# A hybrid decoder trunk on one core: sample products on GpSimd, branch A in plain float32, small copies on ScalarE

## The reference, cut to what matters

```
hn = rmsnorm(x, norm1_g) * (1 + sc1) + sh1
xr, yr, ga, gb, gate_a, gate_b = split(hn @ w_in)
xc, rc_new = causal_depthwise_conv(xr, rc_state, rg_conv_w, rg_conv_b)       # 4 taps
hseq, h_last = rg_lru(xc, h_state, ...)
ya = (gelu(yr) * hseq) @ w_branch_a
u = ga * sigmoid(gb)
v, cc_new = causal_depthwise_conv(u, cc_state, cc_dw_w, cc_dw_b)             # 31 taps
v = silu(layernorm(v, cc_ln_g, cc_ln_b))
yb = v @ w_branch_b + b_branch_b
m = sigmoid(gate_a) * ya + sigmoid(gate_b) * yb
x = x + (1 + g1) * (m @ w_out)
```

## Time and profile before

| | |
|---|---|
| median of 3 runs | 1541.03 us |
| the profiled execution | 1540.55 us |
| its span in the trace | 1538.7 us |
| TensorE matmul busy | 1349.4 us (88%) |
| VectorE busy | 890.1 us (58%) |
| ScalarE busy | 440.7 us (29%) |
| GpSimd busy | 326.2 us (21%) |
| mean granted TensorE clock | 0.936 |

### The profile page before, as it was taken

One profiled execution on the slowest core, in us unless ns is written; L12 is line 12 of the kernel. 1 busy time (PEld: TensorE's weight loads), 2 busy tenths in 40 slices (PEclk: granted clock), 3 DMA queues, 4 the chain that ended last, 5 costly groups with the idle time before them and its releaser, 6 DMA issues.

```text
span 1538.7 us, 28763 instructions
## 1 busy us (share of the span) xinstructions
PE 1349.4 (88%) x12262; PEld 1065.0 (69%) x12262; DVE 890.1 (58%) x1583; ACT 440.7 (29%) x669; POOL 326.2 (21%) x145
## 2 busy tenths in 40 slices
PE   4899996479799999995999935896899999999996
PEld 2798896379699898995997935895454444555443
DVE  3587999967744434336999998765212332212324
ACT  4234474142533332324346521422100000000001
POOL 1366667000000000005775840000100000000000
PEclk9899998789999999997999967996799999999998
DMA  9866524824396674435443447278199999999961
GB/s 398 237 241 226 212 79 130 45 96 168 100 383 239 233 256 141 151 103 122 146 151 97 137 97 73 78 238 335 29 380 370 382 385 382 388 370 372 383 253 35
DMA packets 169954, 332.37 MB, mean 216 GB/s; under 512 B 58480, under 2 KB 133616, under 8 KB 161808
## 3 DMA queue, kind: packets, MB, share of 16 engines
q1 hardware_dynamic: 168576, 327.68, 64.3%
q0 software_dynamic: 1296, 3.54, 0.7%
HBM read 326.06 MB, written 5.13 MB: 215 GB/s over the span
## 4 chain that ended last, share of the span: by engine, by line
PE 67%; DVE 29%; DMA 2%; ACT 1%; issue 1%; POOL 0%; DVEq 0%; SPq 0%; ACTq 0%
PE ps L741 17%; PE ps L542 11%; PE ps L543 10%; PE ps L544 10%; DVE ps L1084 9%; PE ps L765 8%; DVE prod L1105 4%; PE ps L568 2%; PE ps L729 2%; PE ps L584 2%; DVE v L1106 2%; PE ps L576 1%; DVE ps L1081 1%; DMA raw<-in_stream 1%; DVE xc L1250 1%
## 5 line engine op out<-in xcount | busy, mean ns | idle before, releaser
L542 PE MATMUL ps<-xn_hi,whi 128*128 128x320 f32 x1248 | 393.8, 316 | 36.7 <-DVE xn_lo L1032 33.8
L496 POOL TENSOR_TENSOR wlo<-raw,whi 128x1024 fp32r<-128x1024 f32 x104 | 295.5, 2861 | 612.5 <-ACT whi L798 612.5
L543 PE MATMUL ps<-xn_lo,whi 128*128 128x320 f32 x1248 | 388.8, 312 | 0.0
L544 PE MATMUL ps<-xn_hi,wlo 128*128 128x320 f32 x1248 | 388.6, 311 | 0.0
L798 ACT ACTIVATE whi<-raw 128x1024 fp32r<-128x1024 f32 x210 | 221.2, 1056 | 230.1 <-PE ps L544 175.2
L542 PEld LDWEIGHTS ps<-xn_hi,whi 128*128 128x128 f32 x1248 | 237.1, 190 | 54.5 <-issue 33.3
L543 PEld LDWEIGHTS ps<-xn_lo,whi 128*128 128x128 f32 x1248 | 237.4, 190 | 0.2
L544 PEld LDWEIGHTS ps<-xn_hi,wlo 128*128 128x128 f32 x1248 | 237.1, 190 | 0.0
L1032 DVE TENSOR_TENSOR wlo<-raw,whi 128x1024 fp32r<-128x1024 f32 x106 | 128.7, 1221 | 146.2 <-ACT whi L798 146.1
L1084 DVE SCALAR_TENSOR_TENSOR ps<-upad,cols,ps 128x256 f32<-128x256 f32 x464 | 183.5, 478 | 0.0
L542 PE MATMUL ps<-q_hi,whi 128*128 128x320 f32 x256 | 85.8, 335 | 92.5 <-DVE q_lo L1032 58.1
(11 more groups left out here) (232 smaller groups left out, 1510.3 us busy)
## 6 DMA issues: line engine op xcount, KB each, us to landing
raw<-in_stream SPq DMA_DIRECT2D x210, 512.0 KB, 3.7
gbuf<-in_moe SPq DMA_DIRECT2D x36, 1408.0 KB, 13.2
dbuf<-in_moe SPq DMA_DIRECT2D x36, 1408.0 KB, 14.6
ubuf<-in_moe SPq DMA_DIRECT2D x36, 1408.0 KB, 15.2
ada<-in_ada SPq DMA_DIRECT2D x24, 2048.0 KB, 8.3
out_cc<-upad SPq DMA_DIRECT2D x18, 120.0 KB, 13.1
wrg<-in_wrg SPq DMA_DIRECT2D x2, 1024.0 KB, 20.5
upad<-in_cc SPq DMA_DIRECT2D x16, 120.0 KB, 3.4
```

The source lines that it names most:

```text
L496: e.tensor_tensor(wlo[:, s, :], raw[:, s, :], whi[:, s, :].bitcast(F32), ALU.subtract).then_inc(lo_pool, 1)
L542: e.matmul(out, w[0], x2[0], start=start, stop=False)
L543: e.matmul(out, w[0], x2[1], start=False, stop=False)
L544: return e.matmul(out, w[1], x2[0], start=False, stop=stop)
```

## The change

- **Products of the samples.** `conv_samples` is split. GpSimd forms the products for four sequences at a time (`product`, 128x992, 16 per layer) between its subtractions, after the chunks listed in `PROD_AT`. VectorE keeps the sums (`sample_sum`, 16 per layer), placed between taps. `prod` is now two buffers of half the size. Product n waits for the sum of product n - 2, and sum n for product n.
- **Branch A.** Chunks 48 to 55 are `PLAIN`. TensorE multiplies `raw` by `gy` directly, both float32 (`plain`). `high`, `low` and `chunk_low` skip these chunks, q isn't split, and a slot of `raw` is free only when TensorE has done the chunk. Results go to `xc` instead of `gy`.
- **ScalarE.** It takes the samples' bias (8 activations of 128x64 per layer, after chunk 47's evacuation) and the rclast copies (after the gates' sigmoids).
- **Order.** ScalarE's 8 bias activations signal `v_pair`; TensorE waits for `conv_step` ahead of `stat(v)`; `make_u` 4 and 7 move; the sums of a pair are no longer followed by `finish_pair`.

```
-POOL_CHUNKS = 52
+POOL_CHUNKS = 56
+PROD_AT = ((9, 12, 13, 15, 17, 19, 21, 23, 26, 27, 29, 31, 33, 35, 37, 38),
+           (10, 13, 15, 17, 20, 22, 24, 27, 30, 31, 33, 35, 38, 41, 43, 44))
+PLAIN = [any(b + BA <= c < b + BB for b in C_LAYER) for c in range(NCHUNK)]
...
         def split_ready(e, c):
-            if ON_POOL[c]:
+            if PLAIN[c]:
+                e.wait_ge(chunk_done, c + 1)
+            elif ON_POOL[c]:
                 e.wait_ge(lo_pool, LOW_N[c])
...
+            def product(l, h):
+                i, b0 = h // 2, h % 2 * (NB // 2)
+                n = 2 * NT * l + h
+                e.wait_ge(u_made, NT * l + i + 1)
+                if n >= 2:
+                    e.wait_ge(prod_summed, n - 1)
+                a = upad[:, i, PC + TP + b0 * (PC + TS):]
+                window = bass.AP(a.tensor, a.offset, [list(a.ap[0]), [PC + TS, NB // 2], [1, TS], [1, KC]])
+                w0 = _COL["ccw", l] + i
+                taps = cols[:, w0:w0 + (KC - 1) * NT + 1:NT].unsqueeze(1).unsqueeze(1).broadcast_to(
+                    [P, NB // 2, TS, KC])
+                e.tensor_tensor(prod[:, n % 2, :, :].rearrange("p (b t) k -> p b t k", b=NB // 2), window, taps,
+                                ALU.mult).then_inc(prod_made, 1)
+            def mixer(l, c0):
+                b = C_LAYER[l]
+                e.wait_ge(rc_in, 16 * 2 * NT * (l + 1))
+                for c in range(c0, POOL_CHUNKS):
+                    low(b + c, b + c + 1)
+                    if c in PROD_AT[l]:
+                        product(l, PROD_AT[l].index(c))
...
+            def plain(a, b, buf, ready):
+                for c in range(a, b):
+                    s = c % RING
+                    e.wait_ge(raw_landed[s], 16 * (c // RING + 1))
+                    bank_free(e, c)
+                    for k in range(NT):
+                        if c == a:
+                            e.wait_ge(*ready(k))
+                        mm = e.matmul(ps[s][:, 0:T], raw[:, s, k * P:(k + 1) * P], buf[:, k, :], start=k == 0,
+                                      stop=k == NT - 1)
...
+                for p in range(4):
+                    e.wait_ge(prod_summed, 2 * NT * l + 4 * (p + 1))
+                    for i in (2 * p, 2 * p + 1):
+                        ins = e.activation(v[:, i, TP:T], v[:, i, TP:T], ACT.Identity, bias=col("ccb", l, i))
+                    ins.then_inc(v_pair, 1)
+                e.wait_ge(q_ready, 2 * l + 2)
                 for j in range(6):
-                    evac(b + BA + j, gy[:, j, :], ACT.Copy)
+                    evac(b + BA + j, xc[:, j, :], ACT.Copy)
                     high(b + BA + j + RING)
...
+            def sample_sum(l, h):
+                i, t0 = h // 2, TP + h % 2 * (NB // 2 * TS)
+                n = 2 * NT * l + h
+                e.wait_ge(prod_made, n + 1)
+                e.tensor_reduce(v[:, i, t0:t0 + NB // 2 * TS], prod[:, n % 2, :, :], AX.X, ALU.add
+                                ).then_inc(prod_summed, 1)
...
-                conv_samples(l, 0)
                 make_u(6)
-                conv_samples(l, 1)
-                finish_pair(l, 0)
-                e.wait_ge(u_made, NT * l + 4)
-                conv_pair(l, 1, {2: lambda: make_u(7)})
+                make_u(7)
                 e.wait_ge(u_made, NT * (l + 1))
+                sample_sum(l, 1)
+                conv_pair(l, 1, {5: lambda: sample_sum(l, 2), 12: lambda: sample_sum(l, 3),
+                                 20: lambda: sample_sum(l, 4), 28: lambda: sample_sum(l, 5)})
...
-                        link(e.tensor_tensor(half(gy), half(gy), half(xc), ALU.mult))
-                        link(e.tensor_copy(half(q_hi), half(gy)))
-                        low(1, half(q_lo), half(q_hi), half(gy)).then_inc(q_ready, 1)
+                        e.tensor_tensor(half(gy), half(gy), half(xc), ALU.mult).then_inc(q_ready, 1)
```

More of the change, by code:

```diff
@@ L57 @@
 SRC = [*_ORDER, *range(GU, DN + NF), *(C_LAYER[1] + n for n in _ORDER)]
-POOL_CHUNKS = 52
-ON_POOL = [any(b <= c < b + POOL_CHUNKS for b in C_LAYER) for c in range(NCHUNK)]
-LOW_N = [sum(ON_POOL[k] == ON_POOL[c] for k in range(c + 1)) for c in range(NCHUNK)]
+POOL_CHUNKS = 56
+PROD_AT = ((9, 12, 13, 15, 17, 19, 21, 23, 26, 27, 29, 31, 33, 35, 37, 38),
+           (10, 13, 15, 17, 20, 22, 24, 27, 30, 31, 33, 35, 38, 41, 43, 44))
+PLAIN = [any(b + BA <= c < b + BB for b in C_LAYER) for c in range(NCHUNK)]
+ON_POOL = [any(b <= c < b + POOL_CHUNKS for b in C_LAYER) and not PLAIN[c] for c in range(NCHUNK)]
+LOW_N = [sum(ON_POOL[k] == ON_POOL[c] and not PLAIN[k] for k in range(c + 1)) for c in range(NCHUNK)]
+HI_N = [sum(not PLAIN[k] for k in range(c + 1)) for c in range(NCHUNK)]
 MCH = 8 * 352
@@ L159, in build @@
         v = place("v", [P, NT, T], F32)
-        prod = place("prod", [P, NB * TS, KC], F32)
+        prod = place("prod", [P, 2, NB // 2 * TS, KC], F32)
         assert at[0] <= 229344, at[0]
@@ L506, in _ @@
             pads()
-            low(4, POOL_CHUNKS)
+            low(4, 9)
+            mixer(0, 9)
             c1 = C_LAYER[1]
@@ L511, in _ @@
             pads()
-            low(c1 + 4, c1 + POOL_CHUNKS)
+            low(c1 + 4, c1 + 10)
+            mixer(1, 10)
             e.wait_ge(m_ready, 2 * NT)
@@ L916, in _ @@
                                      ).then_inc(rg_sig, 1)
+                e.wait_ge(xc_ready, 4 * (l + 1))
+                e.wait_ge(rc_in, 16 * 2 * NT * (l + 1))
+                if l:
+                    e.wait_ge(out_done, STORES * l)
+                e.activation(rclast[:, :, 0, :], xrp[:, :, TP:TP + PR], ACT.Copy)
+                e.activation(rclast[:, :, 1:, :], xrp[:, :, PR + TP:].rearrange(
+                    "p i (b t) -> p i b t", b=NB)[:, :, :, TS:TS + PR], ACT.Copy).then_inc(st_ready, 1)
+                e.wait_ge(rg_sig, 2 * NT * (l + 1))
                 e.wait_ge(st_ready, 2 * l + 1)
-                e.wait_ge(rg_sig, 2 * NT * (l + 1))
                 for j in range(4):
@@ L1097, in conv_pair @@
                             col("ccb", l, i), k, acc, 2)
-            def conv_samples(l, i):
-                a = upad[:, i, PC + TP:]
-                window = bass.AP(a.tensor, a.offset, [list(a.ap[0]), [PC + TS, NB], [1, TS], [1, KC]])
-                n = _COL["ccw", l] + i
-                taps = cols[:, n:n + (KC - 1) * NT + 1:NT].unsqueeze(1).unsqueeze(1).broadcast_to([P, NB, TS, KC])
-                link(e.tensor_tensor(prod[:].rearrange("p (b t) k -> p b t k", b=NB), window, taps, ALU.mult))
-                link(e.tensor_reduce(v[:, i, TP:T], prod[:], AX.X, ALU.add))
-            def finish_pair(l, p):
-                e.wait_ge(conv_step, conv_n[0])
-                out = v[:, 2 * p:2 * p + 2, TP:T]
-                e.tensor_tensor(out, out, cv("ccb", l, NT)[:, 2 * p:2 * p + 2].unsqueeze(2).broadcast_to(
-                    [P, 2, NB * TS]), ALU.add).then_inc(v_pair, 1)
+            def sample_sum(l, h):
[4 more added lines that the diff above has]
+                                ).then_inc(prod_summed, 1)
             def short_pair(l, p):
```

58 lines of the change are left out of this document (27 added, 31 removed).

## The result

The changed kernel takes 1548.27 us (median of 10 runs, 1545.81 to 1551.85), the kernel before on the same chip 1542.02 us (10 runs, 1540.13 to 1544.82). The ratio is 1.0039, 95% interval 1.0026 to 1.0053: **slower by 0.4%**, where the forecast was 1516 us and the range 1503 to 1540.

The account below looks back on a forecast made before the run. Each layer was taken as TensorE-bound through chunk 47, then a tail where TensorE waits for VectorE. First q_hi of branch B moves -10.9 us in layer 0, -13.7 in layer 1: 1540.55 - 24.6 = 1516 us, range 1503 to 1540.

Parts of the forecast that it names:

- The product's price (p = 3.6): Time of one sample product on GpSimd, absent from the trace: 3.6 us, bounds 2.3 and 6.3.
- rivals 2 and 3: GpSimd short of time, product 4 to 5 us: 1536, chance 0.20; GpSimd the bound, from 5.0 us: 1570, chance 0.12.
- GpSimd becomes the bound: Slower rival, chunks 12 to 44: products from 5.0 us make TensorE late; at 6.3 us 1570, chance 0.12.
- Rival 1: Tail: stores delay nothing beyond their issue, chunk 56's load lands 4.9 us sooner in each layer: 1506, chance 0.18.
- Rival 4: No net change: the tail's gain goes into a wait not seen, 1541 us, chance 0.05.
- TensorE's half, layer 0: Chunks 0 to 47: TensorE stalls 6.2 us at chunk 16 and 0.5 at chunk 18, ending 6.7 us later.
- It holds, barely, except once: Layer 0, four chunks: GpSimd needs 16.8 us against TensorE's 17.0, so TensorE stalls only for the fourth product's late sum.
- To q: From square root to q, layer 0: root through at 252.9, then 10.9 us of recurrence, q at 263.8.
- The slow clock: Tail: stat(th) costs 0.7 us more, since TensorE has idled over 10 us and starts at 1.2 GHz.
- Stores ahead of chunk 56's load: Layer 0's tail: store issue takes 17.4 us, load issued at 298.4, landing near 307; mean at 309.5, 15.4 earlier.
- The late end of slot 59: Tail: slot free only after chunk 55's product, so q_hi comes 10.9 us after stat(th) instead of 7.2, 3.8 more.
- Layer 1's front: Layer 1 up to q: TensorE 4.5 us later by chunk 31, root at 890.5, q at 902.7.

Follow-up runs that it names:

- e4: The changed kernel with only the places of VectorE's sums moved, mostly earlier: 1533.02 us, ratio 0.9919 to the kernel before.
- e11: Changed kernel with early stores, moved sums, earlier statistics, layer 1's last products earlier; new against that: layer 0's last two products behind chunks 41 and 43: 1464.46 us.
- e3: The changed kernel with only SyncE's order changed, ten of eleven stores issued earlier, between loads: 1506.75 us, ratio 0.976 to the kernel before.
- e5: The kernel before with only the stores of the states moved earlier, between loads: 1542.69 us, ratio 0.9993.

## Why the prediction was wrong

Counted on the first q_hi of branch B, the forecast was -10.9 us in layer 0 and -24.6 with layer 1; the trace shows +11.0 and +8.1. (Behind layer 1's q_hi another 2 us are won back, so the spans differ by 6.0.) The 32.7 us between forecast and trace lie in four places:

| step | forecast | measured | off by |
|---|---|---|---|
| branch A's start, layer 0 | 263.8 | 279.9 | +16.1 |
| from there to q_hi, layer 0 | 65.3 | 71.1 | +5.8 |
| q_hi of layer 0 to branch A, layer 1 | 562.7 | 564.7 | +2.0 |
| from there to q_hi, layer 1 | 65.3 | 74.1 | +8.8 |

**The product's price (p = 3.6): too high.** It is 3.02 us on average, 2.8 to 3.1 where nothing disturbs it and 5.58 beside the decay. I spent the chances of rivals 2 and 3 on this number, and neither came true; the loss came with a product cheaper than my central value. "GpSimd becomes the bound" was the wrong slower case. Rival 1 expected the load behind the stores sooner, and it landed later. Rival 4, that the tail's gain goes into a wait, came nearest and had 0.05. The range was also drawn wrongly on its own terms: 1541 lies above 1540, so rival 4 belongs to what it leaves out above, 0.19 and not 0.14.

**"TensorE's half, layer 0 ... 6.7 us later": the step that failed.** "It holds, barely, except once" was weighed against GpSimd's throughput in full and against the coupling in one place only. Product n waits for sum n - 2, and I followed that rule for product 3 and no further. It stops TensorE three times. The first cost 7.3 us (forecast 6.2 and 0.5). The second and third, 5.5 and 9.3, stood in the order of the changed kernel in plain sight: sum 8 behind the fourth `short_pair`, sum 13 behind `decay`. Both places have VectorE waiting or busy for 10 us and more. So chunk 39 ended 22.5 us later than before (1.8 of it the execution's later start) where 6.7 were forecast. e4, which only moves sums, gets 15 us back.

**The third stop has a second cause that the sum put at nothing.** I took one price for a product and one for a subtraction. Beside the decay both take about 5 us, and with the sum out of the way (e4) the stop still costs 6.8 of its 9.3 us. e11 removes it by taking two products out of that time.

**The stops also moved the root.** The step "To q" had ScalarE through the square root at 252.9; it was through at 268.7, since its order has `high`s of chunks ahead of the root, and those waited for TensorE. The step had added TensorE's 6.7 us to the root for this reason; with 22.5 in their place it gives the 268.7. In layer 0 the rest was right: the recurrence's product took 2.83 us as charged, and branch A began 11.1 us after the root's end (10.9 forecast).

**The slow clock was counted at stat(th) only.** Each stop of TensorE was followed by a chunk at 1.2 GHz, 2.0 to 2.8 us. In layer 1 this cost branch A another 2.8. stat(th) took 6.7 instead of the 4.3 it takes at full clock, 2.4 more where I had put 0.7, a figure that no row gave.

**Stores ahead of chunk 56's load: the mechanism right, the term too small.** From chunk 51's end to the load's issue 17.4 us were forecast and 19.1 measured (21.3 in layer 1), then 8.6 to landing against 12.1 (10.9 in layer 1). The term was known as the largest of the tail, and I treated it as a size to work out, though it came from SyncE's order alone. e3 shows 41.5 us for it.

**The late end of slot 59 (q_hi behind table and silu): right.** q_hi came 11.1 us after stat(th), 10.9 forecast. That the whole way from the mean is right too (20.0 us, 19.6 forecast) is luck: stat(th) took 1.7 more than charged, but started 1.3 sooner after the mean than before, since it no longer waited for chunk 54. (Two subtractions of this sum are off by 0.1 each: 324.99 - 309.5 is 15.5, and 10.9 - 7.2 is 3.7.)

**Layer 1's front: right within 2.0 us, by luck in part.** The forecast's q at 902.7 less the 10.9 gained in layer 0 and less 329.1 gives the 562.7 of the table. The recurrence began some 2.5 us sooner than that sum has it, and then took 15.3 us to branch A instead of 10.9: its 2560-element product, charged with 2.8 because GpSimd's subtractions were thought gone, took 7.04, and GpSimd subtracted until 904.7 beside it.

## What to carry to other kernels

Where a helper engine gets a ring of buffers with a partner, write down for every step which of the partner's instructions frees the buffer and what the partner does just ahead of it; the throughput sum says nothing about that, and everything queued behind the helper's step stands with it. When an edit frees a buffer later (here a slot read by the multiply itself instead of by its split), look at which queue entries stood in the hole that closes: stores that cost nothing there turned into 41 us. And a stage that the edit shortens should have its fixed order (after how many chunks a statistic is taken) set anew, which was worth another 17 us here.

## What the runs showed of the hardware

GpSimd and VectorE slowed each other down where both had instructions with two float32 inputs in SBUF. GpSimd's and VectorE's timelines in layer 1 of the changed kernel:

```profile
863.38 3.01 POOL L528 TENSOR_TENSOR prod<-upad,cols 128x992 f32<-128x992 f32 x1
...
873.94 5.58 POOL L528 TENSOR_TENSOR prod<-upad,cols 128x992 f32<-128x992 f32 x1
879.49 9.90 POOL L508 TENSOR_TENSOR wlo<-raw,whi 128x1024 fp32r<-128x1024 f32 x2
```

```profile
872.22 4.44 DVE L1283 TENSOR_TENSOR bb<-bb,xc 128x2560 f32<-128x2560 f32 x1
876.70 5.51 DVE L1284 TENSOR_TENSOR xc<-ab 128x2560 f32<-128x2560 f32 x1
882.25 4.91 DVE L1285 SCALAR_TENSOR_TENSOR th<-xc,th 128x2560 f32<-128x2560 f32 x1
...
900.33 7.04 DVE L1290 TENSOR_TENSOR bb<-bb,th 128x2560 f32<-128x2560 f32 x1
```

Beside the decay a product takes 5.58 us instead of 3.01, and two subtractions 9.90 instead of 4.8; VectorE's operations of 2560 elements take 4.4 to 7.0 where the same line with GpSimd idle takes 2.83 (L1290 in layer 0). The taps beside GpSimd's work, which have one of their two tiles in PSUM, keep their 0.48 us. The Trainium skill names it too: "GPSIMD Engine Reference", section Specifications, has GpSimd's SBUF interfaces shared with VectorE, with contention for VectorE's instructions with two SBUF inputs. The rows look like taking turns, each instruction waiting until the other engine's has ended. In layer 0 a subtraction of 5.02 us ends at 231.28, L1284, which started at 229.04, ends 2.7 us later, and L1285 behind it, with GpSimd idle, takes 2.83. This is read from rows; no run tests it. L1284 squares one tile with itself; in no trace here does it run without a subtraction beside it, so its own length isn't shown. So what moves from VectorE to GpSimd should stay clear of VectorE's wide SBUF operations; e11 shows what two products less there are worth (TensorE's wait of 5.0 us gone, and the time 5.0 us less, 1469.48 to 1464.46).

A store in short pieces is dear on SyncE's queue: eight stores of 120 KB each (128 x 8 pieces of 30 floats) held it for 17.0 and 19.3 us in the changed kernel, some 2 us each, and the engines moved 41 to 47 GB/s from 305 to 320 us. Spread over the loads of 16 chunks each took 0.4 to 1.0 us of the queue (e3, e5) and held nothing up.

What stays open: why the load's landing behind the stores differs (12.1 and 10.9 us), how much of the slow-clock time a filled hole would give back, and what ScalarE's bias and copies are worth alone; none of it was tried.
